# First query weights split by VectorE in free output-weight buffers, first expert blocks and keys loaded during the mixer's back part, and matmuls of ones in four waits of TensorE

## What is computed

```python
h = _rms(x) * (1.0 + scale1) + shift1            # shift, scale, gate from c
proj = h @ w_in[l]                                # cut into the parts of both head groups
mixed = jnp.concatenate([sb_out, gla_out], axis=-1) @ w_out[l]
x = x + gate1 * mixed
h2 = _rms(x) * (1.0 + scale2) + shift2
# peer_layer(h2):
q = (h @ w_q).reshape(t_tot, PEER_HEADS, PEER_QUERY_DIM)
s1 = jnp.einsum('thd,hkd->thk', q1, keys_a); s2 = jnp.einsum('thd,hkd->thk', q2, keys_b)
# top 16 of each, top 16 of the sums, softmax of them as gates, then per token
act = gelu(h . expert_u[idx]);  y = sum(gate * act * expert_v[idx])
x = x + gate2 * y;  out = _rms(x) * g_final
```

## Time and profile before

| | us |
|---|---|
| median of 3 runs | 1612.54 |
| the profiled execution, whole | 1613.84 |
| its span, first to last instruction | 1612.1 |
| TensorE busy | 1551.9 (96%) |
| VectorE busy | 1289.8 (80%) |
| ScalarE busy | 713.5 (44%) |
| GpSimd busy | 387.1 (24%) |
| mean granted TensorE clock | 0.987 |

### The profile page before, as it was taken

One profiled execution on the slowest core, in us unless ns is written; L12 is line 12 of the kernel. 1 busy time (PEld: TensorE's weight loads), 2 busy tenths in 40 slices (PEclk: granted clock), 3 DMA queues, 4 the chain that ended last, 5 costly groups with the idle time before them and its releaser, 6 DMA issues.

```text
span 1612.1 us, 23400 instructions
## 1 busy us (share of the span) xinstructions
PE 1551.9 (96%) x8161; PEld 1364.5 (85%) x8161; DVE 1289.8 (80%) x2612; ACT 713.5 (44%) x1124; POOL 387.1 (24%) x328
## 2 busy tenths in 40 slices
PE   6999998979999999999999999999999999999997
PEld 3787665769899999999999999998888888888886
DVE  6766655358599999999999999767888888888887
ACT  4322765254334333434577767534333333333333
POOL 0000001323233233323122222122333333333310
PEclk9999999989999999999999999999999999999999
DMA  8754002036777888789798899899999999999982
GB/s 334 270 214 150 27 1 105 26 120 211 242 260 241 282 281 272 234 266 318 230 321 320 309 331 323 314 318 343 344 352 355 356 353 355 356 348 366 345 297 101
DMA packets 176965, 426.86 MB, mean 265 GB/s; under 512 B 15168, under 2 KB 99280, under 8 KB 172112
## 3 DMA queue, kind: packets, MB, share of 16 engines
q1 hardware_dynamic: 139984, 291.14, 51.6%
q0 software_dynamic: 36864, 134.23, 23.8%
HBM read 372.88 MB, written 52.43 MB: 264 GB/s over the span
## 4 chain that ended last, share of the span: by engine, by line
PE 72%; DMA 1%; DVE 1%; ACT 0%; issue 0%; DVEq 0%; ACTq 0%
PE ps_y L1975 11%; PE ps_y L1979 11%; PE ps_y L1977 11%; PE ps_u L1183 10%; PE ps_u L1184 10%; PE ps_u L1185 10%; PE ps_g L1678 5%; PE ps_q L1365 1%; PE ps_q L1367 1%; PE ps_q L1366 1%; DMA activations<-u_act 1%; PE ps_s L1377 1%; PE ps_u L2010 0%; DVE y_scaled L1921 0%; DVE row L1942 0%
## 5 line engine op out<-in xcount | busy, mean ns | idle before, releaser
L1183 PE MATMUL ps_u<-h_hi,u_hi 128*128 128x384 f32 x1024 | 349.0, 341 | 3.2 <-DVE u_lo L1173 1.7
L1185 PE MATMUL ps_u<-h_hi,u_lo 128*128 128x384 f32 x1024 | 344.9, 337 | 0.0
L1184 PE MATMUL ps_u<-h_lo,u_hi 128*128 128x384 f32 x1024 | 344.7, 337 | 0.0
L1846 ACT CAST v_hi<-v_raw 128x1024 fp32r<-128x1024 f32 x128 | 134.7, 1052 | 326.1 <-issue 323.5
L1242 POOL DMA_INDIRECT row<-in_v,row_index x128 | 172.5, 1348 | 377.9 <-DVE h_row L1262 317.8
L1242 POOL DMA_INDIRECT row<-in_u_rows,row_index x128 | 150.5, 1176 | 448.9 <-DVE row_dots L1249 378.3
L1904 DVE TENSOR_TENSOR v_lo<-v_raw,v_hi 128x1024 fp32r<-128x1024 f32 x128 | 160.4, 1253 | 101.9 <-ACT v_hi L1846 101.9
L1975 PE MATMUL ps_y<-v_hi,w_hi 128*128 128x512 f32 x768 | 237.9, 390 | 0.3 <-DVE w_lo L1891 0.3
L1979 PE MATMUL ps_y<-v_hi,w_lo 128*128 128x512 f32 x768 | 237.1, 389 | 0.0
L1977 PE MATMUL ps_y<-v_lo,w_hi 128*128 128x512 f32 x768 | 237.0, 389 | 0.0
L1173 DVE TENSOR_TENSOR u_lo<-u_raw,u_hi 128x1024 fp32r<-128x1024 f32 x128 | 167.0, 1310 | 74.8 <-ACT u_hi L1166 74.7
(11 more groups left out here) (304 smaller groups left out, 2296.4 us busy)
## 6 DMA issues: line engine op xcount, KB each, us to landing
u_raw<-in_u SPq DMA_DIRECT2D x128, 512.0 KB
v_raw<-in_v SPq DMA_DIRECT2D x128, 512.0 KB
w_ada<-in_w_ada SPq DMA_DIRECT2D x24, 1024.0 KB, 7.2
activations<-u_act SPq DMA_DIRECT2D x128, 192.0 KB
gate_tiles<-g_tile SPq DMA_DIRECT2D x12, 2048.0 KB
gates<-gate_tiles SPq DMA_DIRECT2D x32, 768.0 KB, 8.5
act<-activations SPq DMA_DIRECT2D x128, 192.0 KB
w_proj<-in_w_proj SPq DMA_DIRECT2D x16, 512.0 KB, 4.7
```

What stands on the lines that cost most here:

```text
L1183: pe.matmul(out, self.hi[n][:, k], hi, start=(k == 0), stop=False)
L1184: pe.matmul(out, self.hi[n][:, k], lo, start=False, stop=False)
L1185: last = pe.matmul(out, self.lo[n][:, k], hi, start=False, stop=(k == KD - 1))
```

## The change

Five things are done.

1. A new helper `keep_warm(pe, ones, bank, count)` issues `count` float32 matmuls of a 128x128 matrix of ones with itself into a PSUM bank that nobody reads at that time. It is called with 5 and 8 after `mod_columns(0)` and `mod_columns(1)`; with 4 in each of the steps `d = 16, 17, 18` of `stick_breaking`, where TensorE first waits for the last kept projection; with 8 at the start of `mixer_back`; and with 18 after the second sum of squares there, ahead of the first query product.
2. The first head's query weights are split inside the loop over `n` of the output projection, after `n = 5` and `n = 6`: ScalarE copies them into the slots of `w_hi` that are free by then, and VectorE instead of GpSimd subtracts, into `w_lo`.
3. SyncE loads blocks 0 and 1 of `u` and the keys of head 0 at the start of `mixer_back` instead of at the start of `retrieval`. For that their buffers and semaphores are made before `gated_linear`, and four small constants give their place back earlier.
4. In `retrieval` SyncE starts with the query weights of head 1 and blocks 2 on.
5. In `retrieval` ScalarE copies blocks 0 and 1 (`up.high`) ahead of `keep_scores(0)`.

```diff
+def keep_warm(pe, ones, bank, count):
+    for n in range(count):
+        pe.matmul(bank[:, 0:P], ones[:], ones[:], start=True, stop=True)
...
             mod_columns(0)
+            keep_warm(pe, keep["ones"], ps_v[0], 5)
             mod_columns(1)
+            keep_warm(pe, keep["ones"], ps_v[0], 8)
...
                 if d < PARTS * BESIDE:
                     beside(d)
+                if d == ND:
+                    pe.wait_ge(proj.kept, N_PROJ)
+                if d >= ND:
+                    keep_warm(pe, keep["ones"], ps_f, 4)
...
-        wq, wq_hi, wq_lo = halves(catT), halves(cat_hi), halves(cat_lo)
+        wq = halves(catT)
+        wq_hi, wq_lo = [[w[n % WS][:] for n in FIRST_QUERY_AT] for w in (w_hi, w_lo)]   # (KD - 3, KD - 2)
...
         def _(sp):
+            for b in range(up.FIRST):
+                up.load(sp, b)
+            for s in range(2):
+                sp.dma_start(query["keys"][s][:], io[("keys_a", "keys_b")[s]][0]).then_inc(query["keys_in"][s], 16)
             sp.wait_ge(clo, KD)
...
-            act.wait_ge(wq_in, 32)
-            act.wait_ge(mix_done, KD)
-            act.copy(wq_hi[0], wq[0]).then_inc(query["hi"], 1)
+                if n in FIRST_QUERY_AT:
+                    s = FIRST_QUERY_AT.index(n)
+                    act.wait_ge(wq_in, 32)
+                    act.wait_ge(mix_done, n + 1)
+                    act.copy(wq_hi[s], wq[s]).then_inc(query["hi"], 1)
...
-            act.copy(wq_hi[1], wq[1]).then_inc(query["hi"], 1)
...
-            for s in range(2):
-                pool.wait_ge(query["hi"], s + 1)
-                pool.tensor_tensor(wq_lo[s], wq[s], wq_hi[s].bitcast(F32), ALU.subtract).then_inc(query["lo"], 1)
...
         def _(pe):
+            keep_warm(pe, keep["ones"], ps_p[2], 8)
...
+            pe.wait_ge(x_done, KD - 2)
+            keep_warm(pe, keep["ones"], ps_p[2], 18)
             pe.wait_ge(query["lo"], 2)
...
+                if n in FIRST_QUERY_AT:
+                    s = FIRST_QUERY_AT.index(n)
+                    dve.wait_ge(query["hi"], s + 1)
+                    dve.tensor_tensor(wq_lo[s], wq[s], wq_hi[s].bitcast(F32), ALU.subtract).then_inc(query["lo"], 1)
...
-            load_keys(0)
-            for b in range(2):
-                up.load(sp, b)
             load_query(1)
-            for b in range(2, up.DEEP):
+            for b in range(up.FIRST, up.DEEP):
                 up.load(sp, b)
...
             for s in range(2):
                 keep_query(0, s)
+            for b in range(up.FIRST):
+                up.high(act, b)
             keep_scores(0)
-            for b in range(up.AHEAD):
+            for b in range(up.FIRST, up.AHEAD):
                 up.high(act, b)
             query_high(1)
```

More of the change, by code:

```diff
@@ L947, in _, with mixer_back @@
                             last.then_inc(inter, 1)
-def mixer_back(nc, io, keep, t16, v8, gx, catT, query):
+def mixer_back(nc, io, keep, t16, v8, gx, catT, query, up):
     with ExitStack() as ctx:
@@ L961, in mixer_back @@
         NG = KD - TB
+        FIRST_QUERY_AT = (KD - 3, KD - 2)
         cat = lambda c0, c1: catT[:, c0:c1] if c1 <= TB else t16[:, SBQ + c0 - TB:SBQ + c1 - TB]
@@ L1133, with __init__, buffers @@
 class UpProducts:
-    RING, LEAD, AHEAD, DEEP = 4, 2, 3, 6
-    def __init__(self, nc, ctx, io, keep, acts):
+    RING, LEAD, AHEAD, DEEP, FIRST = 4, 2, 3, 6, 2
+    def __init__(self, nc, ctx, io, keep):
+        sem = lambda n: ctx.enter_context(nc.semaphore(n))
+        self.io, self.keep = io, keep
+        span = range(self.RING)
+        self.raw = [ctx.enter_context(nc.sbuf_tensor(f"u_raw{n}", [P, KD, P], F32)) for n in range(self.FIRST)]
+        self.u_in, self.stored = [sem(f"u_in{n}") for n in span], [sem(f"act_stored{n}") for n in span]
+        self.hi_done, self.lo_done, self.mul, self.act_done = sem("u_hi_done"), sem("u_lo_done"), sem("u_mul"), sem("u_act_done")
+    def buffers(self, nc, ctx, acts):
         sb = lambda n, s, d=F32: ctx.enter_context(nc.sbuf_tensor(n, s, d))
-        sem = lambda n: ctx.enter_context(nc.semaphore(n))
-        self.io, self.keep, self.acts = io, keep, acts
+        self.acts = acts
         span = range(self.RING)
-        self.raw = [sb(f"u_raw{n}", [P, KD, P]) for n in span]
+        self.raw += [sb(f"u_raw{n}", [P, KD, P]) for n in range(self.FIRST, self.RING)]
         self.splits = ctx.enter_context(ExitStack())
@@ L1150, in __init__ @@
         self.ps = [ctx.enter_context(nc.psum_tensor(f"ps_u{n}", [P, T], F32)) for n in range(2)]
-        self.u_in, self.stored = [sem(f"u_in{n}") for n in span], [sem(f"act_stored{n}") for n in span]
-        self.hi_done, self.lo_done, self.mul, self.act_done = sem("u_hi_done"), sem("u_lo_done"), sem("u_mul"), sem("u_act_done")
     def load(self, sp, b):
@@ L1277, in retrieval @@
         w_lo = [sb(f"w_query_lo{s}", [P, KD, P], F32R) for s in range(2)]
-        keys = [sb(f"keys{s}", [P, N_KEYS]) for s in range(2)]
+        keys, k_in = query["keys"], query["keys_in"]
         q = [sb(f"query{s}", [P, T]) for s in range(2)]
@@ L1301, in retrieval @@
         iota_done, ident_done, h_turned, h_kept = sem("iota50_done"), sem("ident_r_done"), sem("h_turned"), sem("h_row_kept")
-        w_in, k_in = [sem(f"wq_in{s}") for s in range(2)], [sem(f"keys_in{s}") for s in range(2)]
+        w_in = [sem(f"wq_in{s}") for s in range(2)]
         wq_hi, wq_lo, q_done = query["hi"], query["lo"], query["done"]
@@ L1314, in load_keys @@
                 for s in range(2):
-                    if h > 0:
-                        sp.wait_ge(s_done, h)
+                    sp.wait_ge(s_done, h)
                     sp.dma_start(keys[s][:], io[("keys_a", "keys_b")[s]][h]).then_inc(k_in[s], 16)
@@ L2039, in program @@
             msb = lambda n, s, d=F32: mix.enter_context(nc.sbuf_tensor(n, s, d, side="right"))
-            for n, d in (("neg_ones_r", F32R), ("neg_tri_r", F32R), ("ident_b", BF16), ("future", BF16)):
-                keep[n] = msb(n, [P, P], d)
             for n in ("h_hi", "h_lo"):
@@ L2045, in program @@
             with ExitStack() as weights:
+                for n, d in (("neg_ones_r", F32R), ("neg_tri_r", F32R), ("ident_b", BF16), ("future", BF16)):
+                    keep[n] = weights.enter_context(nc.sbuf_tensor(n, [P, P], d))
                 proj = Projections(nc, weights, io)
@@ L2051, in program @@
                 stick_breaking(nc, io, keep, t16, v8, catT, operands, proj)
+            up = UpProducts(nc, top, io, keep)
+            keys = [sb(f"keys{s}", [P, N_KEYS]) for s in range(2)]
             out_weights = mix.enter_context(ExitStack())
@@ L2060, in program @@
                 **{n: top.enter_context(nc.semaphore(f"query_{n}")) for n in ("hi", "lo", "done")},
+                "keys": keys, "keys_in": [top.enter_context(nc.semaphore(f"keys_in{s}")) for s in range(2)],
             }
-            mixer_back(nc, io, keep, t16, v8, gx, catT, query)
+            mixer_back(nc, io, keep, t16, v8, gx, catT, query, up)
         acts = nc.dram_tensor("activations", [N_KEYS, P, DENSE], F32, kind="Internal").ap()
         g_stored = [top.enter_context(nc.semaphore(f"g_stored{n}")) for n in range(2)]
-        up = UpProducts(nc, top, io, keep, acts)
+        up.buffers(nc, top, acts)
         rows = PickedRows(nc, top, io)
```

## The result

Beside each other, five runs each, the kernel before takes 1612.45 us (1610.54 to 1614.52) and the changed one 1602.73 (1597.59 to 1604.73): a ratio of 0.9933, 95% interval 0.9917 to 0.9948. The profiled execution took 1603.31 us, 10.5 less than that of before. Forecast were 1602.3 and 1603.6.

The account below looks back on a forecast made before the run. TensorE, busy 96%, was taken as the bound, so an earlier start of its expert blocks ends earlier. 0 + 2.5 - 0.3 + 3.8 + 4.2 = 10.2 us: profiled 1603.6, median 1602.3; 8-in-10 range 1599.5 to 1608.3.

Parts of the forecast that it names:

- Front: Front stage: its five and eight matmuls of ones neither cost nor win, 0 us; bounds -0.7 to 0.
- Matmul of ones: Price of one wherever added: 0.22 us at full clock, 0.45 at half as upper bound.
- End of the stick-breaking: End of `stick_breaking`: ones hold the clock for `suffix` and `outputs`, +2.5 us; -0.3 if four are too few.
- Start of `mixer_back`: Eight ones ahead of the first sums: -0.3 us taken, 0 at full clock, -1.4 at half.
- Query weights in the loop: Output projection in `mixer_back`: splitting the first query weights there is hidden behind TensorE, 0 us; 1.3 if not covered.
- End of `mixer_back`: First query product starts 1.9 us earlier and at full clock: +3.8 us, 2.1 of it the clock.
- `retrieval`: Start of `retrieval`: first expert block earlier (2.5 us) and clock held (1.65): 4.2 us taken, 4.3 at most.
- The 4.0 us wait: TensorE's later wait on GpSimd moves along with TensorE and keeps its length, so earlier gains survive.
- ones without effect: Rival: the ones don't hold the clock, so only 4.2 us are won: 1608.3; chance 0.13.
- Late weights: Rival in `retrieval`: head 1's weights leave GpSimd ready 2.3 us after TensorE: 1604.6; chance 0.10.
- a gain given back: Rival: `retrieval`'s 4.2 us are lost at the later 4.0 us wait: 1606.5; chance 0.11.
- Dear ones: Rival: a matmul of ones costs far more; at 0.9 us each, 1626.2; chance 0.02.

Follow-up runs that it names:

- e12: The changed kernel without the front stage's five and eight matmuls of ones: 1602.36 us, ratio 0.9943 to the kernel before.
- e6: The changed kernel with 36 instead of 18 matmuls of ones at the end of `mixer_back`: 1604.04 us, ratio 0.9945 to the kernel before.
- e1: The changed kernel without any matmul of ones: 1606.42 us, ratio 0.9965 to the kernel before.
- e4: The kernel before with only the early loads and ScalarE's new order in `retrieval`: 1604.54 us, ratio 0.9959.
- e3: The kernel before with only the first query weights split inside the loop by VectorE: 1610.53 us, ratio 0.9990.
- e11: The changed kernel without the eighteen matmuls of ones at the end of `mixer_back`: 1603.31 us, ratio 0.9953 to the kernel before.
- e2: The kernel before with all the matmuls of ones and nothing else: 1608.86 us, ratio 0.9983.
- e9: The changed kernel as it is, timed again in a later series: 1602.08 us, ratio 0.9944 to the kernel before.
- e7: The changed kernel without the eight ones starting `mixer_back`, with ten ending `gated_linear`'s TensorE work instead: 1600.16 us, ratio 0.9919 to the kernel before.
- e5: The changed kernel without the eight matmuls of ones at the start of `mixer_back`: 1599.13 us, ratio 0.9914 to the kernel before.

## Why the prediction was right

*Front, 0 us*: right; e12 shows it (0.3 us between the medians).

*Matmul of ones, 0.22 at full and 0.45 at half clock*: 0.23 for the 18, 0.22 for the 18 more of e6, 0.47 for the eight.

*End of the stick-breaking, +2.5*: 12.89 - 10.56 = 2.33. The parts are as forecast: the `suffix` at full clock, `outputs` at 2.38, and the last four cost 0.3 (from the end of `outputs` to the next block 1.38 us, 1.06 before). That four of ones hold the clock was the open point; no trace with them shows it fallen (1.00 from 234 to 248 in all ten). The gain is against the state of the earlier trace rows: in e1 and e4, without ones, `outputs` ran at full clock too and only 1.1 to 1.2 us were left to win: about half of this term depends on how long the low stretch lasts in the execution that it is compared with.

*Start of `mixer_back`, -0.3*: the one term that was mis-sized. It was -1.5, a little beyond the lower bound of -1.4, since all eight ran at half clock (0.50 from 266 to 270): the clock had fallen in the gap of 2.64 us ahead of the block (1.00 up to 265.75, 0.50 from 266.0; the gap ends at 266.62). The text named this gap and then weighed it too lightly, and where it weighs the rival it says that the gaps left are 1.4 us and less, which leaves this one out. Nothing before the eight held the clock. Six of seven traces with the eight give the 1.5, e6 0.4.

*Query weights in the loop, 0*: right; from the block's start to the second sum e3 takes 57.28 us, before 57.26.

*End of `mixer_back`, +3.8*: 20.79 - 17.05 = 3.74. The split's share is as forecast (second sum to the first product 7.35 us before, 5.54 after: 1.8). The clock's 1.9 are against the earlier trace rows; e11, e1 and e3 give 1.2, 2.2 and 2.6 for it. With GpSimd's subtraction beside them VectorE's two scaled rows take 4.10 us (e2), without it 1.42 (e3). In before, e2 and e4 the second of the two rows ends 0.54, 0.55 and 0.55 us after GpSimd's second subtraction. (For slow rows of another origin the prediction gives 8.4 as its sum; 10.2 less 1.9 is 8.3.)

*`retrieval`, +4.2*: 17.42 - 13.14 = 4.28; first block at T + 4.76 (T + 4.9 forecast), head 1's query at T + 13.1 (13.2), block 2's copy at T + 7.1 (8.3), and no wait for GpSimd.

*The 4.0 us wait keeps its length*: right in the pair of profiles, and `row_index` moved with TensorE. It is not a constant, though: 3.2 to 4.1 in the other traces, and 0.3 in e2. The gathers that GpSimd issues ahead of these weights differ from one execution to the next: the eighth took 3.97 us in before and 0.94 in e2. A run that isolates this was not made.

The terms as measured are 0.15 (the copy of the last projection comes at 234.45, 234.60 in the earlier trace rows) + 2.33 - 1.53 + 3.74 + 4.28 = 9.0, and 10.5 were won. The missing 1.5 are the stretch at 286 us, low in the profile of before and not in that of the changed kernel; the forecast had allowed 1.7 either way for such a piece. First before, then the changed kernel:

```profile
286.00:290.00 4.00, 3.80 (x10) 2.93 (x11) 1.59 (x3) 1.66 (x3) 2.37 (x1) 0.60 0.52 185
```

```profile
286.00:290.00 4.00, 4.00 (x19) 3.29 (x18) 1.44 (x4) 1.81 (x3) 2.89 (x2) 1.00 0.71 262
```

e9, the same kernel, has it low. So the mechanism was right in every other term, but that the profiled time fell within 0.3 us of the forecast is luck: this piece and the mis-sized term cancel. By the terms alone the change is worth 9.0 us; the medians gave 9.7 and, in e9, 9.0.

The rivals: ones without effect is refuted by e1 and e11. Late weights and a gain given back don't occur in any trace: head 1's query is 13.13 to 13.14 us behind T wherever the loads are early, and the later wait is never above 4.1. Dear ones are refuted by e6.

## What to carry to other kernels

Filling an idle gap of TensorE paid where real work of TensorE on the critical path started right behind it (1.1 to 2.3 us at the end of the stick-breaking, 1.2 at the end of `mixer_back` by e11), and the fill is best begun when the last work ends: put behind a gap of 2.6 us, it ran at half clock itself for all or most of its length and delayed what followed by 0.4 to 1.5 us, while e7's ten, begun at once, left the clock at 1.00. Where another engine set the pace behind the gap, a held clock bought nothing: in e7 the logarithm is at 3.99 and the second sum at 55.75, as without it in e5 (3.99 and 55.76). When a term has a known bound and the text names the reason why it may be reached, as the unfilled gap here, size the term at that bound.

## What the hardware showed

The same program can have a stretch at half clock in one execution and not in another. The changed kernel had the clock at 1.00 from 286 to 290 us in one profiled execution and at 0.60 in another, with the waits of TensorE ahead of it the same to 0.1 us. `outputs` without ones took 4.06 us in before and 3.80 in e3, but 2.37 in e1 and 2.38 in e4. That is 1.4 to 1.7 us for each place.

Two more such places lie outside what the change touches. One is at 132 us in the front stage, behind eight matmuls of one column and four of 16 rows, with no idle time of TensorE before it. First e9, which has it, then e11, which doesn't (the programs differ only by the 18, some 190 us later):

```profile
132.00:136.00 4.00, 4.00 (x12) 3.04 (x11) 0.00 (x0) 1.02 (x2) 0.00 (x0) 0.57 0.58 236
```

```profile
132.00:136.00 4.00, 3.12 (x14) 2.31 (x14) 0.97 (x2) 1.82 (x3) 0.00 (x0) 1.00 0.63 254
```

Ten of the 14 executions have it; their last projection is copied at 233.8 to 234.8 us, in the other four at 232.7 to 233.0. The other place is near 776 us, in six of the 14, again e9 and not e11:

```profile
776.00:780.00 4.00, 2.69 (x12) 2.69 (x13) 3.90 (x6) 0.95 (x2) 0.00 (x0) 0.66 0.54 162
```

```profile
776.00:780.00 4.00, 3.38 (x23) 3.38 (x24) 3.97 (x6) 0.26 (x1) 0.00 (x0) 1.00 0.51 173
```

The wait before head 2's query has one behind it too (0.61 from 396 to 400 in the changed kernel), in all but e1 and e2. These two and the waits explain the last column of the table: less TensorE's waits of 3.2 to 8.0 us it is 1238.4 without a low stretch (e1), 1239.7 to 1239.9 with one (eight executions), 1241.4 to 1241.6 with two (e6, e7, e9, e12), and 1242.5 in e3, where the first of the two is longer.

The runs of one kernel spread accordingly: 1602.74 to 1617.46 for 35 of the kernel before in one series. A difference of 2 us between two medians of six runs is hardly a finding here. The time between two marks of the trace can be one: wherever the clock is the same, it repeats to 0.1 us (58.83 to 58.91, 17.04 to 17.09, 13.13 and 13.14).
